# The products of p for the third and fourth column groups, moved behind their gates' products at the end of a one-core transformer block

## The chip, the cores and the metric

One core of a Trainium2 chip runs the whole program. The time is that of the device, in microseconds (us), for one execution. Of three timed runs of the kernel before, the median is 1574.86 us (1574.80 to 1574.87). The trace is of one further, profiled execution, which took 1574.96 us.

## The reference, cut to what matters

A decoder layer over 256 tokens and 2048 channels in float32: three token mixers, their gates and an output projection, then a gated MLP with a short convolution, and last a gated input embedding. Only the last step is touched, and the weights and products behind it:

```python
x = x + merged @ w_out[i]                                # (256, 2048)
h = rms_norm(x, norm_ffn_g[i])
u = causal_dwconv(h @ w_up[i], ffn_conv_w[i])
u_g, u_v = jnp.split(u, 2, axis=-1)
x = x + (jax.nn.silu(u_g) * u_v) @ w_down[i]
g = jax.nn.sigmoid(rms_norm(x, norm_ple_g[i]) @ w_ple_gate[i])   # (256, 2048) @ (2048, 2048)
x = x + g * (p[i] @ w_ple[i])                            # p: (256, 256), w_ple: (256, 2048)
```

The kernel computes the sigmoid as (1 + tanh(z/2)) / 2.

## The kernel before

All weights stream through a ring of four buffers in chunks of 128 partitions x 1024 columns (512 KB): two blocks of 128 input rows by 512 output columns. For each chunk c, in this order: SyncE issues its DMA into `raw` once chunk c-4 has been split (`chunk`, L334 to L340); ScalarE casts it to fp32r, `w_hi` (`high`, L894), once the DMA has landed and TensorE has used chunk c-4; VectorE computes the rest `w_lo = raw - w_hi` (`split`, L1215) and counts up `chunk_split`; TensorE waits for that count and runs 12 matmuls of 512 columns on it (`token_chunk`, L502 to L518: two token tiles x two row blocks x the products high-high, high-low, low-high), or 16 and 16 in the stages of the MLP's first projection, and counts up `chunk_used`.

Every engine runs its own list of instructions in the order in which the program is written. The lists are written by hand as loops over the chunk number: the work that belongs to a stage is put behind the cast or the split of a certain chunk. So a wait in such a piece of work holds up all later casts or splits of that engine.

A column group is 512 output columns; there are four. The products of a group are summed in one of two PSUM accumulators, `acc[number % 2]`, and the group two later in TensorE's order must wait until it has been read (`wait_taken`). The last stages are:

- Behind the output projection, near 735 us: four chunks "ple", one for each column group, with the products p @ w_ple. ScalarE copies each to SBUF, halved, into the tile `ple` (L954). `p_hi` and `p_lo` are the two parts of p, transposed.
- The MLP in two halves (UP1, DOWN1, UP2, DOWN2).
- From chunk PLEG on: four gate groups of eight chunks each with h @ w_ple_gate. END is the number of all chunks. Below, E-1 is the last chunk, E-2 the one before, and so on, so that a chunk can be named alike in both kernels. ScalarE takes the tanh of groups 0 to 2 behind a cast (L1174), that of group 3 for each token tile apart when its products are done (L1183). VectorE computes (tanh + 1) * ple into `fin` (L1704) and adds x (L1706); for group 3 tile by tile (L1711, L1713). `fin` has two buffers, for even and odd groups.
- SyncE issues the eight output DMAs (256 KB each, two for each column group) behind the DMAs of all weight chunks (L402). Each group's two count up `out_landed[g % 2]`. VectorE waits for the landing of group 0's output before it writes group 2's into the same buffer of `fin`.

## Time and profile before

| what | value |
|---|---|
| median of three timed runs | 1574.86 us |
| the profiled execution | 1574.96 us, its span 1573.0 us |
| TensorE matmuls busy | 1565.7 us, 100% of the span |
| VectorE busy | 1047.2 us, 67% |
| ScalarE busy | 780.9 us, 50% |
| chain that ended last | 99% TensorE |
| DMA | 297.16 MB, mean 189 GB/s |

The span is the time from the first to the last record of the profiled execution; 1.96 us of the execution's own time lie around it. Matmuls overlap, so a row with 390 ns for one is issued every 227 ns. Columns of a row of the timeline: start in us, length in us, engine, line, operation, out<-in, count, and in brackets the engine's idle time before it and what ended it.

### The profile page before, as it was taken

What the parts mean: (1) busy time and instruction counts of PE and PEld (TensorE: products, weight loads), DVE (VectorE), ACT (ScalarE), POOL (GpSimd) and SP (SyncE); (2) the same over time, 40 slices, a digit from 0 to 9 for tenths busy, and PEclk for the clock granted to TensorE, in tenths of its full rate; (3) what the DMA queues carried; (4) which work ended last, traced back from release to release, by engine and by line L of the source; (5) the groups of instructions that cost most, each with busy time, mean ns of one, the idle gap of its engine ahead of it and who ended that gap; (6) DMA issues with size and microseconds to landing.
All of it is one profiled execution on the core that took longest, in us unless ns stands there. A gap on an engine that the chain in (4) does not pass through costs nothing.

```text
span 1573.0 us, 21349 instructions
## 1 busy us (share of the span) xinstructions
PE 1565.7 (100%) x7740; PEld 1323.6 (84%) x7740; DVE 1047.2 (67%) x1238; ACT 780.9 (50%) x928; POOL 34.7 (2%) x53
## 2 busy tenths in 40 slices
PE   9999999999999999999999999999999999999998
PEld 7878888888888888888888888888888888888887
DVE  5699867765677556655677777764457777765554
ACT  7355454444554544455455555543345555544443
POOL 5000110000000000000000000000000000000000
PEclk9999999999999999999999999999999999999999
DMA  8656655665655666655666566656666666566564
GB/s 261 201 174 191 196 176 168 196 187 180 194 180 174 197 198 194 187 187 174 188 187 200 173 187 196 191 199 191 196 178 198 180 181 199 192 193 190 177 197 147
DMA packets 157074, 297.16 MB, mean 189 GB/s; under 512 B 9639, under 2 KB 14099, under 8 KB 157008
## 3 DMA queue, kind: packets, MB, share of 16 engines
q1 hardware_dynamic: 156464, 296.00, 61.3%
q8 instruction: 43, 0.70, 0.2%
q0 software_dynamic: 512, 0.27, 0.1%
q14 instruction: 23, 0.19, 0.0%
q10 hardware_dynamic: 32, 0.01, 0.0%
HBM read 294.14 MB, written 2.10 MB: 188 GB/s over the span
## 4 chain that ended last, share of the span: by engine, by line
PE 99%; DVE 0%; ACT 0%; issue 0%; POOL 0%; ACTq 0%; DVEq 0%; POOLq 0%
PE psum L513 21%; PE psum L515 21%; PE psum L514 21%; PE psum L486 20%; PE psum L492 11%; PE psum L678 0%; PE psum L625 0%; PE psum L579 0%; PE psum L689 0%; PE psum L712 0%; PE psum L534 0%; PE psum L647 0%; PE psum L666 0%; PE psum L656 0%; PE psum L568 0%
## 5 line engine op out<-in xcount | busy, mean ns | idle before, releaser
L1215 DVE TENSOR_TENSOR w_lo<-raw,w_hi 128x1024 fp32r<-128x1024 f32 x547 | 666.0, 1223 | 439.7 <-ACT w_hi L894 438.8
L894 ACT CAST w_hi<-raw 128x1024 fp32r<-128x1024 f32 x547 | 571.3, 1049 | 605.0 <-PE psum L515 461.7
L513 PE MATMUL psum<-w_hi,h_both 128*128 128x512 f32 x860 | 340.2, 396 | 0.0
L486 PE MATMUL psum<-h_both,w_hi 128*128 128x512 f32 x1408 | 336.4, 391 | 0.0
L515 PE MATMUL psum<-w_hi,h_both 128*128 128x512 f32 x860 | 335.1, 390 | 0.0
L514 PE MATMUL psum<-w_lo,h_both 128*128 128x512 f32 x860 | 335.0, 390 | 0.0
L486 PEld LDWEIGHTS psum<-h_both,w_hi 128*128 128x128 f32 x1408 | 258.7, 188 | 50.3 <-DVE rB L1595 0.3
L515 PEld LDWEIGHTS psum<-w_hi,h_both 128*128 128x128 f32 x860 | 161.5, 188 | 34.4
L513 PEld LDWEIGHTS psum<-w_hi,h_both 128*128 128x128 f32 x860 | 161.6, 188 | 33.0 <-issue 0.5
L514 PEld LDWEIGHTS psum<-w_lo,h_both 128*128 128x128 f32 x860 | 161.7, 188 | 31.9
L492 PEld LDWEIGHTS psum<-h_both,w_lo 128*128 128x128 f32 x1408 | 180.6, 191 | 6.9
L492 PE MATMUL psum<-h_both,w_lo 128*128 128x256 f32 x1408 | 182.9, 283 | 0.0
L513 PE MATMUL psum<-w_hi,f_hi 128*128 128x512 f32 x352 | 137.2, 390 | 0.0
L515 PE MATMUL psum<-w_hi,f_lo 128*128 128x512 f32 x352 | 137.0, 389 | 0.0
L514 PE MATMUL psum<-w_lo,f_hi 128*128 128x512 f32 x352 | 137.0, 389 | 0.0
L514 PEld LDWEIGHTS psum<-w_lo,f_hi 128*128 128x128 f32 x352 | 66.1, 188 | 13.7
L513 PEld LDWEIGHTS psum<-w_hi,f_hi 128*128 128x128 f32 x352 | 66.1, 188 | 13.7
L515 PEld LDWEIGHTS psum<-w_hi,f_lo 128*128 128x128 f32 x352 | 66.1, 188 | 13.6
L1304 DVE SCALAR_TENSOR_TENSOR val<-apad,cw,val 128x256 f32<-128x256 f32 x120 | 50.2, 480 | 1.0
L513 PE MATMUL psum<-w_hi,m_hi 128*128 128x512 f32 x128 | 50.2, 392 | 0.0
L514 PE MATMUL psum<-w_lo,m_hi 128*128 128x512 f32 x128 | 49.8, 389 | 0.0
L515 PE MATMUL psum<-w_hi,m_lo 128*128 128x512 f32 x128 | 49.8, 389 | 0.0
(274 smaller groups left out, 1079.1 us busy)
## 6 DMA issues: line engine op xcount, KB each, us to landing
raw<-in_w_up SPq DMA_DIRECT2D x176, 512.0 KB, 3.7
raw<-in_w_gate SPq DMA_DIRECT2D x96, 512.0 KB, 3.7
raw<-in_w_in SPq DMA_DIRECT2D x90, 512.0 KB, 3.7
raw<-in_w_down SPq DMA_DIRECT2D x88, 512.0 KB, 4.5
raw<-in_w_out SPq DMA_DIRECT2D x32, 512.0 KB, 3.8
raw<-in_w_ple_gate SPq DMA_DIRECT2D x32, 512.0 KB, 4.6
raw<-in_w_moba_out SPq DMA_DIRECT2D x16, 512.0 KB, 4.1
raw<-in_w_conv_out SPq DMA_DIRECT2D x8, 512.0 KB, 4.1
```

The source lines that it names most:

```text
L486: mm = nc.tensor.matmul(wide[part][:, j, :], w_hi[:, c % RING, w], h_both[:, kt + k, :, :].rearrange("p h s -> p (h s)"), start=first and ...
L492: mm = nc.tensor.matmul(wide[part][:, j, S:2 * S], w_lo[:, c % RING, w], h_hi[:, kt + k, :], start=False, stop=last and not low_first and ...
L513: nc.tensor.matmul(o, sh, w_hi[:, c % RING, w], start=first and k == 0, stop=False, skip_group_check=True)
L514: nc.tensor.matmul(o, sh, w_lo[:, c % RING, w], start=False, stop=False, skip_group_check=True)
L515: mm = nc.tensor.matmul(o, sl, w_hi[:, c % RING, w], start=False, stop=last and k == 1, skip_group_check=True)
L894: A.copy(w_hi[:, c % RING, :], raw[:, c % RING, :]).then_inc(chunk_high, 1)
L1215: V.tensor_tensor(w_lo[:, c % RING, :], raw[:, c % RING, :], w_hi[:, c % RING, :].bitcast(F32), ALU.subtract).then_inc(chunk_split, 1)
L1304: last = V.scalar_tensor_tensor(val[:, j, :], src, w, val[:, j, :], ALU.mult, ALU.add)
```

## The change

The loop over the "ple" chunks behind the output projection is cut from four groups to two (column groups 0 and 1). The chunks of w_ple for groups 2 and 3 now stand at the end: one behind the eight gate chunks of group 2 (`PLE2`, E-10) and one as the last chunk of the program (E-1). The number of chunks stays the same, so END is unchanged, PLEG and UP1 are two lower, and a chunk of the last stage that was PLEG+n is now PLEG+n+2 at the same place from the end. `GATE_AT` holds the first chunk of each gate group.

TensorE sums the moved products in the accumulator that follows their gate's; they are not copied out, but VectorE multiplies them in PSUM by the gate. For that, it first turns the tanh of groups 2 and 3 into the gate, (tanh + 1) * 0.5, in `gt2`, which has two buffers now. p's parts move to an address that stays free until the end; `ple` holds half its columns. On SyncE the loop with a register over the gate chunks becomes a written-out list.

```diff
@@ -68,7 +68,7 @@
                                 ("gv", 1, 8), ("gr", 1, 8), ("mq", 1, 8), ("mk", 1, 8),
                                 ("mq2", 1, 8), ("mk2", 1, 8), ("mv", 2, 8), ("yA", 4, 2),
                                 ("gA", 4, 8), ("yB", 4, 2), ("gB", 4, 8), ("yC", 4, 4),
-                                ("gC", 4, 8), ("wout", 4, 8), ("ple", 4, 1)):
+                                ("gC", 4, 8), ("wout", 4, 8), ("ple", 2, 1)):
         for g in range(count):
             GROUPS.append((name, g, c, chunks))
             c += chunks
...
@@ -82,7 +82,9 @@
 UP2 = DOWN1 + 4 * K1 // 2
 DOWN2 = UP2 + 16 * PAIRS2
 PLEG = DOWN2 + 4 * K2 // 2
-END = PLEG + 32
+PLE2 = PLEG + 24
+END = PLEG + 34
+GATE_AT = (PLEG, PLEG + 8, PLEG + 16, PLE2 + 1)
 GROUP_AT = {}
 for _n, (_name, _g, _c0, _k) in enumerate(GROUPS):
     for _j in range(_k):
...
@@ -210,8 +212,8 @@
     pT = ar("pT", [P, 2, 3 * P], 78)
     m_hi = ar("m_hi", [P, KD, S], 32, F32R)
     m_lo = ar("m_lo", [P, KD, S], 48, F32R)
-    p_hi = ar("p_hi", [P, 2, S], 64, F32R)
-    p_lo = ar("p_lo", [P, 2, S], 66, F32R)
+    p_hi = ar("p_hi", [P, 2, S], 80.5, F32R)
+    p_lo = ar("p_lo", [P, 2, S], 82.5, F32R)
     ptok = ar("ptok", [P, TT, PLE], 76)
     sqx = ar("sqx", [P, TT, W], 0)
     upg = ar("upg", [P, QD, 2 + S], 0)
...
@@ -221,8 +223,8 @@
     tg = ar("tg", [P, QD, S], 16.5)
     f_hi = ar("f_hi", [P, K1, S], 20.5, F32R)
     f_lo = ar("f_lo", [P, K1, S], 44.5, F32R)
-    ple = ar("ple", [P, TT, D], 68.5)
-    gt2 = ar("gt2", [P, TT, W], 8.5)
+    ple = ar("ple", [P, TT, 2 * W], 68.5)
+    gt2 = ar("gt2", [P, 2, TT, W], 8.5)
     fin = ar("fin", [P, 2, TT, W], 36.5)
 
     psum = nc.alloc_psum_tensor("psum", [P, 8, 512], F32)
...
@@ -390,11 +392,11 @@
         down(DOWN1, K1, 0)
         up(UP2, PAIRS2, PAIRS1)
         down(DOWN2, K2, K1)
-        with sp.Fori(0, 2) as i:
-            for half in range(2):
-                for j in range(8):
-                    chunk(PLEG + 8 * half + j,
-                          w_ple_gate[0][j * 256:(j + 1) * 256, bass.ds(i * 2 * W + half * W, W)], 2, i, 16)
+        for g in range(4):
+            for j in range(8):
+                chunk(GATE_AT[g] + j, w_ple_gate[0][j * 256:(j + 1) * 256, g * W:(g + 1) * W], 2)
+            if g >= 2:
+                chunk(GATE_AT[g] + 8, w_ple[0][:, g * W:(g + 1) * W], 2)
         for g in range(4):
             for t in range(TT):
                 if t == 0 or g == 3:
...
@@ -513,7 +515,7 @@
                     nc.tensor.matmul(o, sh, w_hi[:, c % RING, w], start=first and k == 0, stop=False, skip_group_check=True)
                     nc.tensor.matmul(o, sh, w_lo[:, c % RING, w], start=False, stop=False, skip_group_check=True)
                     mm = nc.tensor.matmul(o, sl, w_hi[:, c % RING, w], start=False, stop=last and k == 1, skip_group_check=True)
-                if c == END - 1 and t < TT - 1:
+                if c in (END - 2, END - 1) and t < TT - 1:
                     mm.then_inc(tile0_sums, 1)
             mm.then_inc(chunk_used, 1)
 
...
@@ -854,16 +856,27 @@
                 token_chunk(DOWN2 + g * n + j, number % 2, f_hi, f_lo, 2 * j, j == 0, j == n - 1)
                 if g and j == 1:
                     turn_x(g - 1, number - 1, U_X2 + g - 2 if g >= 3 else None)
-        for g in range(4):
-            number = NG_PLEG + g
+        def ple_gate(g, number):
+
             wait_taken(pe, number - 2)
             for j in range(8):
-                c = PLEG + 8 * g + j
                 if g == 0 and j % 2 == 0:
                     pe.wait_ge(unit_split, U_X2 + j // 2 + 1)
-                token_chunk(c, number % 2, h_hi, h_lo, 2 * j, j == 0, j == 7)
+                token_chunk(GATE_AT[g] + j, number % 2, h_hi, h_lo, 2 * j, j == 0, j == 7)
                 if g == 0 and j == 1:
                     turn_x(3, number - 1, U_X2 + 2)
+
+        def ple_sums(c, number):
+
+            wait_taken(pe, number - 2)
+            token_chunk(c, number % 2, p_hi, p_lo, 0, True, True)
+
+        ple_gate(0, NG_PLEG)
+        ple_gate(1, NG_PLEG + 1)
+        ple_gate(2, NG_PLEG + 2)
+        ple_sums(PLE2, NG_PLEG + 3)
+        ple_gate(3, NG_PLEG + 4)
+        ple_sums(END - 1, NG_PLEG + 5)
 
 
     @block.scalar
...
@@ -1168,19 +1181,19 @@
                     number = NG_PLEG + g
                     act.wait_ge(chunk_used, PLEG + 8 * g + 8)
                     act.wait_ge(r2_ready, 1)
-                    if g:
-                        act.wait_ge(pg_ready, g)
+                    if g == 2:
+                        act.wait_ge(pg_ready, 1)
                     for t in range(TT):
-                        last = A.activation(gt2[:, t, :], flat(acc[number % 2])[:, t * W:(t + 1) * W], ACT.Tanh,
+                        last = A.activation(gt2[:, g % 2, t, :], flat(acc[number % 2])[:, t * W:(t + 1) * W], ACT.Tanh,
                                             scale=small[:, 14 - t:15 - t])
                     last.then_inc(taken[number % 2], 1)
-        act.wait_ge(pg_ready, 3)
+        act.wait_ge(pg_ready, 2)
         for t in range(TT):
             if t == 0:
                 act.wait_ge(tile0_sums, 1)
             else:
-                act.wait_ge(chunk_used, END)
-            A.activation(gt2[:, t, :], flat(acc[(NG_PLEG + 3) % 2])[:, t * W:(t + 1) * W], ACT.Tanh,
+                act.wait_ge(chunk_used, GATE_AT[3] + 8)
+            A.activation(gt2[:, 1, t, :], flat(acc[(NG_PLEG + 4) % 2])[:, t * W:(t + 1) * W], ACT.Tanh,
                          scale=small[:, 14 - t:15 - t]).then_inc(tile_gate, 1)
 
 
...
@@ -1586,7 +1599,7 @@
                 if c == LAST["wout", g] + 5:
                     earlier()
                     x_low(g, U_X1 + g, R_FFN)
-            if c == UP1 + 1:
+            if c == UP1 + 3:
                 earlier()
                 x_mean(5)
             if c == UP1 + 10:
...
@@ -1694,22 +1707,38 @@
                 dve.wait_ge(rs_ready, 9)
                 V.tensor_scalar(small[:, 14:15], ms[:, 0:1], 0.5, None, ALU.mult)
                 V.tensor_scalar(small[:, 13:14], ms[:, 1:2], 0.5, None, ALU.mult).then_inc(r2_ready, 1)
-            for g in range(3):
+            for g in range(2):
                 if c == PLEG + 8 * g + (14 if g == 0 else 12):
                     number = NG_PLEG + g
                     cols = slice(g * W, (g + 1) * W)
                     wait_taken(dve, number)
-                    if g >= 2:
-                        dve.wait_ge(out_landed[g % 2], 16 * TT)
-                    V.scalar_tensor_tensor(fin[:, g % 2, :, :], gt2[:], 1.0, ple[:, :, cols], ALU.add, ALU.mult).then_inc(pg_ready, 1)
+                    V.scalar_tensor_tensor(fin[:, g, :, :], gt2[:, g, :, :], 1.0, ple[:, :, cols], ALU.add, ALU.mult).then_inc(pg_ready, 1)
                     dve.wait_ge(pg_ready, g + 1)
-                    V.tensor_tensor(fin[:, g % 2, :, :], fin[:, g % 2, :, :], xtok[:, :, cols], ALU.add).then_inc(out_ready, 1)
+                    V.tensor_tensor(fin[:, g, :, :], fin[:, g, :, :], xtok[:, :, cols], ALU.add).then_inc(out_ready, 1)
+            if c == PLEG + 28:
+                wait_taken(dve, NG_PLEG + 2)
+                V.tensor_scalar(gt2[:, 0, :, :], gt2[:, 0, :, :], 1.0, 0.5, ALU.add, ALU.mult).then_inc(gate_halved, 1)
+            if c == PLEG + 29:
+                cols = slice(2 * W, 3 * W)
+                dve.wait_ge(chunk_used, PLE2 + 1)
+                dve.wait_ge(gate_halved, 1)
+                dve.wait_ge(out_landed[0], 16 * TT)
+                V.tensor_tensor(fin[:, 0, :, :], tokens(acc[(NG_PLEG + 3) % 2]), gt2[:, 0, :, :], ALU.mult).then_inc(taken[(NG_PLEG + 3) % 2], 1)
+                wait_taken(dve, NG_PLEG + 3)
+                V.tensor_tensor(fin[:, 0, :, :], fin[:, 0, :, :], xtok[:, :, cols], ALU.add).then_inc(out_ready, 1)
         cols = slice(3 * W, 4 * W)
+        for t in range(TT):
+            dve.wait_ge(tile_gate, t + 1)
+            V.tensor_scalar(gt2[:, 1, t, :], gt2[:, 1, t, :], 1.0, 0.5, ALU.add, ALU.mult).then_inc(gate_halved, 1)
         dve.wait_ge(out_landed[1], 16 * TT)
         for t in range(TT):
-            dve.wait_ge(tile_gate, t + 1)
-            V.scalar_tensor_tensor(fin[:, 1, t, :], gt2[:, t, :], 1.0, ple[:, t, cols], ALU.add, ALU.mult).then_inc(pg_ready, 1)
-            dve.wait_ge(pg_ready, 4 + t)
+            if t == 0:
+                dve.wait_ge(tile0_sums, 2)
+            else:
+                dve.wait_ge(chunk_used, END)
+            dve.wait_ge(gate_halved, 2 + t)
+            V.tensor_tensor(fin[:, 1, t, :], flat(acc[(NG_PLEG + 5) % 2])[:, t * W:(t + 1) * W], gt2[:, 1, t, :], ALU.mult).then_inc(pg_ready, 1)
+            dve.wait_ge(pg_ready, 3 + t)
             V.tensor_tensor(fin[:, 1, t, :], fin[:, 1, t, :], xtok[:, t, cols], ALU.add).then_inc(out_ready, 1)
 
     block.__exit__(None, None, None)
```

What the diff does to VectorE's list around the wait for group 0's output, behind the additions of gate group 1 (L1706, after: L1717). The splits are L1215 before and L1228 after; `gt_118` is the tile `gt2`. Before:

```order
L1704 SCALAR_TENSOR_TENSOR fin<-gt_118,ple 128x1024 [waits taken1,chunk_split]
L1706 TENSOR_TENSOR fin<-fin,xtok 128x1024 [waits pg_ready]
L1215 TENSOR_TENSOR w_lo<-raw,w_hi 128x1024 [waits chunk_high]
L1215 TENSOR_TENSOR w_lo<-raw,w_hi 128x1024 [waits chunk_high,chunk_split] x7
L1704 SCALAR_TENSOR_TENSOR fin<-gt_118,ple 128x1024 [waits out_landed0,taken0,chunk_split]
L1706 TENSOR_TENSOR fin<-fin,xtok 128x1024 [waits pg_ready]
L1215 TENSOR_TENSOR w_lo<-raw,w_hi 128x1024 [waits chunk_high]
```

The wait for group 0's output stands behind E-4's split there. The same place in VectorE's list after:

```order
L1717 TENSOR_TENSOR fin<-fin,xtok 128x1024 [waits pg_ready]
L1228 TENSOR_TENSOR w_lo<-raw,w_hi 128x1024 [waits chunk_high]
L1228 TENSOR_TENSOR w_lo<-raw,w_hi 128x1024 [waits chunk_high,chunk_split] x7
L1720 TENSOR_SCALAR gt_118<-gt_118 128x1024 [waits taken0,chunk_split]
L1228 TENSOR_TENSOR w_lo<-raw,w_hi 128x1024 [waits chunk_high]
L1726 TENSOR_TENSOR fin<-psum,gt_118 128x1024 [waits gate_halved,out_landed0,chunk_used,chunk_split]
L1728 TENSOR_TENSOR fin<-fin,xtok 128x1024 [waits taken1]
L1228 TENSOR_TENSOR w_lo<-raw,w_hi 128x1024 [waits chunk_high]
```

Eight splits stand behind group 1's addition in both. Before, the eighth is that of E-4, and the wait on `out_landed0` follows with three splits behind it. Now the eighth is that of E-6, the halving follows, then one split (E-5), then the wait, with four splits behind it.

The end of VectorE's list before, from the last two splits on:

```order
L1215 TENSOR_TENSOR w_lo<-raw,w_hi 128x1024 [waits chunk_high,chunk_split] x2
L1711 SCALAR_TENSOR_TENSOR fin<-gt_118,ple 128x512 [waits chunk_split,out_landed1,tile_gate]
L1713 TENSOR_TENSOR fin<-fin,xtok 128x512 [waits pg_ready]
L1711 SCALAR_TENSOR_TENSOR fin<-gt_118,ple 128x512 [waits tile_gate]
L1713 TENSOR_TENSOR fin<-fin,xtok 128x512 [waits pg_ready]
```

Behind the tanh (`tile_gate`) there are two operations for each tile. The same end after, from the last three splits on (L1732 halves the gate, L1740 multiplies):

```order
L1228 TENSOR_TENSOR w_lo<-raw,w_hi 128x1024 [waits chunk_high,chunk_split] x3
L1732 TENSOR_SCALAR gt_118<-gt_118 128x512 [waits chunk_split,tile_gate]
L1732 TENSOR_SCALAR gt_118<-gt_118 128x512 [waits tile_gate]
L1740 TENSOR_TENSOR fin<-psum,gt_118 128x512 [waits gate_halved,tile0_sums,out_landed1]
L1742 TENSOR_TENSOR fin<-fin,xtok 128x512 [waits pg_ready]
L1740 TENSOR_TENSOR fin<-psum,gt_118 128x512 [waits gate_halved,chunk_used]
L1742 TENSOR_TENSOR fin<-fin,xtok 128x512 [waits pg_ready]
```

Two operations for each token tile stood behind the tanh; now the tanh and the halving of both tiles stand ahead of the two operations that follow the last products.

SyncE's list before, at the last weight chunks and the first outputs (ISA is an instruction that only waits; REGISTER_ALU computes the next address or count):

```order
L339 ISA [waits chunk_split]
L339 DMA raw<-in_w_ple_gate 128x2x512
L336 REGISTER_ALU
L339 ISA [waits chunk_split]
L339 DMA raw<-in_w_ple_gate 128x2x512
L393 REGISTER_ALU
L393 COMPARE_AND_BRANCH
L402 DMA out<-fin 128x512 [waits out_ready]
L402 DMA out<-fin 128x512
L402 DMA out<-fin 128x512 [waits out_ready]
```

Each weight DMA has a waiting instruction and a register step of its own. SyncE's list at the same place after:

```order
L384 COMPARE_AND_BRANCH
L341 DMA raw<-in_w_ple_gate 128x2x512 [waits chunk_split] x24
L341 DMA raw<-in_w_ple 128x2x512 [waits chunk_split]
L341 DMA raw<-in_w_ple_gate 128x2x512 [waits chunk_split] x8
L341 DMA raw<-in_w_ple 128x2x512 [waits chunk_split]
L404 DMA out<-fin 128x512 [waits out_ready]
L404 DMA out<-fin 128x512
L404 DMA out<-fin 128x512 [waits out_ready]
```

The loop's registers and its branch are gone, and the DMA of the last w_ple chunk stands directly ahead of the outputs.

## Rows read from the trace of the kernel before

**Rows 1.** The page: the span, and busy time of TensorE.
```profile
span 1573.0 us, 21349 instructions
...
PE 1565.7 (100%) x7740; PEld 1323.6 (84%) x7740; DVE 1047.2 (67%) x1238; ACT 780.9 (50%) x928; POOL 34.7 (2%) x53
```

**Rows 2.** The timelines of four engines at the end of the span.
```profile
1567.52 0.39 PE L515 MATMUL psum<-w_hi,h_both 128*128 128x512 f32 x1
...
1566.67 0.69 ACT L1183 ACTIVATE gt<-psum,small 128x512 f32<-128x512 f32 x1 [8.67 <-PE psum L515]
1567.94 0.69 ACT L1183 ACTIVATE gt<-psum,small 128x512 f32<-128x512 f32 x1 [0.59 <-PE psum L515]
...
1567.49 0.69 DVE L1711 SCALAR_TENSOR_TENSOR fin<-gt,ple 128x512 f32<-128x512 f32 x1 [5.58 <-ACT gt L1183]
1568.21 0.69 DVE L1713 TENSOR_TENSOR fin<-fin,xtok 128x512 f32<-128x512 f32 x1
...
1569.54 0.69 DVE L1713 TENSOR_TENSOR fin<-fin,xtok 128x512 f32<-128x512 f32 x1
...
1570.26 0.33 SPq L402 DMA_DIRECT2D out<-fin  x1
```

**Rows 3.** The timeline of VectorE, from E-5's split to the last splits.
```profile
1547.22 1.23 DVE L1215 TENSOR_TENSOR w_lo<-raw,w_hi 128x1024 fp32r<-128x1024 f32 x1 [1.49 <-ACT w_hi L894]
1549.91 1.23 DVE L1215 TENSOR_TENSOR w_lo<-raw,w_hi 128x1024 fp32r<-128x1024 f32 x1 [1.47 <-ACT w_hi L894]
1555.77 1.23 DVE L1704 SCALAR_TENSOR_TENSOR fin<-gt,ple 128x1024 f32<-128x1024 f32 x1 [4.64 <-DMA out<-fin]
1557.03 1.22 DVE L1706 TENSOR_TENSOR fin<-fin,xtok 128x1024 f32<-128x1024 f32 x1
1558.17 3.74 DVE L1215 TENSOR_TENSOR w_lo<-raw,w_hi 128x1024 fp32r<-128x1024 f32 x3
```

**Rows 4.** The timeline of the matmuls and weight loads, at the starts of E-4 and E-3.
```profile
1556.66 0.39 PE L513 MATMUL psum<-w_hi,h_both 128*128 128x512 f32 x1
...
1559.44 0.19 PEld L513 LDWEIGHTS psum<-w_hi,h_both 128*128 128x128 f32 x1 [0.32 <-DVE w_lo L1215]
...
1559.79 0.39 PE L514 MATMUL psum<-w_lo,h_both 128*128 128x512 f32 x1
```

**Rows 5.** The groups by line and shape, a VectorE operation reading PSUM.
```profile
L1428 DVE TENSOR_SCALAR ex<-psum 128x512 f32<-128x512 f32 x1 | 0.7, 692 | 0.0
```

**Rows 6.** SyncE's queue: E-1's weights, then the second output of group 0.
```profile
1548.61 0.37 SPq L339 DMA_DIRECT2D raw<-in_w_ple_gate  x1
...
1549.61 0.42 SPq L402 DMA_DIRECT2D out<-fin  x1
```

**Rows 7.** The timelines of VectorE and SyncE in a written-out stretch near 725 us.
```profile
723.26 1.23 DVE L1215 TENSOR_TENSOR w_lo<-raw,w_hi 128x1024 fp32r<-128x1024 f32 x1 [1.49 <-ACT w_hi L894]
...
724.51 0.37 SPq L339 DMA_DIRECT2D raw<-in_w_ple  x1
```

**Rows 8.** The DMA view; KB, us to landing: issues at 1549.19, 1549.61, 1550.57, 1558.28.
```profile
out<-fin SPq DMA_DIRECT2D x1, 256.0 KB, 4.3
...
out<-fin SPq DMA_DIRECT2D x1, 256.0 KB, 6.0
...
out<-fin SPq DMA_DIRECT2D x1, 256.0 KB, 6.4
...
out<-fin SPq DMA_DIRECT2D x1, 256.0 KB, 2.4
```

**Rows 9.** The timeline of ScalarE, at the tanh of gate group 2.
```profile
1546.06 1.05 ACT L894 CAST w_hi<-raw 128x1024 fp32r<-128x1024 f32 x1 [1.67 <-PE psum L515]
1547.15 1.27 ACT L1174 ACTIVATE gt<-psum,small 128x512 f32<-128x512 f32 x2
```

**Rows 10.** Stretches after TensorE's last matmul; the third figure from the end: the granted clock.
```profile
1568.00:1572.00 4.00, 0.00 (x0) 0.00 (x0) 2.17 (x4) 0.63 (x1) 0.00 (x0) 1.00 0.34 131
1572.00:1573.00 1.00, 0.00 (x0) 0.00 (x0) 0.00 (x0) 0.00 (x0) 0.00 (x0) 0.87 0.00 0
```

More of the change, by code:

```diff
@@ L277, in trunk @@
     r2_ready, pg_ready, out_ready = sem("r2_ready"), sem("pg_ready"), sem("out_ready")
-    tile0_sums, tile_gate = sem("tile0_sums"), sem("tile_gate")
+    tile0_sums, tile_gate, gate_halved = sem("tile0_sums"), sem("tile_gate"), sem("gate_halved")
     cv_ready = sem("cv_ready")
```

## The prediction

> **What bounds the kernel now.** I read the page first: TensorE is busy for 1565.7 us of a span of 1573.0 us [rows 1]. Every microsecond taken from another engine is worth nothing unless TensorE waits for it, or it stands behind the last matmul. So two questions decide: does TensorE run through after the change as it does before, and what is left behind its last matmul?
>
> The tail first. The last matmul starts at 1567.52. The tanh of the second token tile starts at 1567.94, VectorE's last addition at 1569.54, and the last output is issued at 1570.26: 2.74 us from the last matmul's start to the issue [rows 2].
>
> Then VectorE's timeline in the last 26 us [rows 3]. Normally it idles 1.49 us ahead of each split, waiting for the cast. After the split of E-4 (1549.91 to 1551.14) it waits 4.64 us for the landing of group 0's output, then multiplies and adds for group 2, and only at 1558.17 goes on to the splits of E-3, E-2 and E-1, 3.74 / 3 = 1.25 us each. E-3's split ends at 1559.42. In TensorE's rows [rows 4] E-4 starts at 1556.66. From the second matmul of E-3 (1559.79) to the last of all (1567.52) are 34 matmuls, 0.2273 us each, or 2.73 us for a chunk of 12. E-3's second matmul was due at 1556.66 + 13 x 0.2273 = 1559.62 and comes at 1559.79, and its weight load has 0.32 us idle ahead of it, put down to the split. So before, the long wait of VectorE already costs TensorE 0.17 us: the cover of three split chunks is used to the last bit.
>
> **The change, part by part.**
>
> TensorE's products: 24 matmuls leave the place behind the output projection and 24 come in at the end, of the same shape. Sum 0. ScalarE loses two copies, VectorE gains halvings: none of it on the path unless shown below. Behind the output projection ScalarE and VectorE do the same work at the same distance from its last chunk, less the two copies; only the MLP's first chunks stand two places nearer. I take 0, with 0 to +1 us as bounds, since one of those chunks could now be wanted before it is split.
>
> The wait on `out_landed0`. This is the term that counts. SyncE issues group 0's output behind E-1's weights, and those wait for E-5's split: the same in both kernels. The landing is therefore at nearly the same time. But VectorE now comes to this wait one split earlier: E-4's split stands behind it, not ahead of it. Queued behind the waiting multiplication are E-4's to E-1's splits, and TensorE waits for the first of them.
>
> Its time: VectorE starts the multiplication at 1555.77 in the trace. Multiplication and addition are both 128x1024 as before; the multiplication now reads PSUM. A 128x512 operation reading PSUM took 0.692 us [rows 5], as long as the 0.69 us of those at the end of VectorE's list that read SBUF [rows 2], so the price is the same. The first split behind them ends at 1559.42, as before, if the landing is the same.
>
> The landing can be a little earlier, because SyncE's loop is written out. In the loop E-1's DMA is issued at 1548.61 [rows 6], 0.16 us after E-5's split ended (1547.22 + 1.23 = 1548.45) [rows 3]; in a written-out stretch the lag is 724.51 - 724.49 = 0.02 us [rows 7]. The second output of group 0 was issued at 1549.61, 1.00 us after E-1's weights; with DMAs of 0.37 and 0.42 us in a row and no branch it would be some 0.8 us. So it is issued 0.14 + 0.2 = 0.34 us earlier, its weights ahead of it 0.14 us. It landed 6.0 us after its issue [rows 8], behind the weights and beside group 1's outputs, so not all of it comes back. Bounds 0 and 0.34; I take 0.25.
>
> So E-4's split ends at 1559.42 - 0.25 = 1559.17. E-3's load came at 1559.44, 0.02 us behind its split, and the second matmul 0.35 us behind the load [rows 4]. So E-4's second matmul comes at 1559.54. It is due at 1556.66 + 0.23 = 1556.89. TensorE loses 2.65 us, against the 0.17 us it loses now: +2.48 us. The later splits are ahead again (1.25 us each against 2.73 us).
>
> Both ends of this term: if the landing is as late as the slowest output of these rows (6.4 us) [rows 8] and SyncE gains nothing, 0.4 + 0.25 more: +3.1 us. If both outputs land like the one that had nothing beside it (2.4 us behind an issue at 1549.3, so 1551.7), the split of E-4 ends at 1551.8 + 1.26 + 1.14 + 1.25 = 1555.4, ahead of E-4's load, and the term is -0.17 us. I take +2.48, since the 6.0 us is of this very DMA with the same traffic ahead and beside it.
>
> The page "DMA: Bandwidth & Descriptors" of the Trainium skill (section "Anatomy of one DMA — SWDGE (gpsimd) path") gives a transfer a fixed part of about 2 us and a part by its bytes; for 256 KB that is an estimate of 2.6 us, for another kind of queue. The rows agree with it for the output that had nothing beside it (2.4 us), and disagree for group 0's (4.3 and 6.0 us). By the page the wait would be gone by 1552 and the change a gain; by the rows it isn't.
>
> The tanh of group 2. Gate group 3 (its first chunk is E-9) now uses the accumulator of group 2, not of group 1, since the p products of group 2 stand between. So E-9's first load waits for the tanh behind E-7's cast. In the trace the pair of tanhs stands behind E-5's cast, 1547.15 to 1548.42 [rows 9]; two chunks earlier it ends at 1542.97. E-9 starts at 1556.66 - 5 x 2.73 = 1543.0, its load is due 0.2 us ahead of that. TensorE would lose some 0.1 us; bounds 0 and 0.2. It shifts the later casts with it, so it isn't hidden by the later wait: +0.1 us.
>
> The halving of group 2, one operation of 128x1024, stands between two splits with 1.49 us idle ahead of each [rows 3]. It is not in the trace; a 128x512 operation took 0.69 us [rows 5], a two-operand one of 128x1024 1.23 us [rows 3]. Both ends fit into the 1.49 us: 0 us. If that cover were gone it would delay E-5's split and with it E-1's weights and the landing.
>
> The tail. Counted from the last matmul's start: the first tile's sums are ready for another engine 0.85 us before it (1567.52 - 1566.67), the second's 0.42 us after it (1567.94) [rows 2]. VectorE multiplies tile 0 at -0.85 and adds at -0.13 (dependent operations stand 0.72 us apart: 1567.49, 1568.21). The multiplication of tile 1 needs its products (+0.42) and VectorE (+0.48 to +0.5, since the 1.33 us from 1568.21 to 1569.54 hold one operation and a dependent one, 0.61 + 0.72). So it starts at +0.5, the addition at +1.22, the output's issue 0.72 us later, at +1.94. Before it was +2.74: -0.8 us. The tanhs and halvings of group 3 lie beside the 2.73 us of E-1: tanh of tile 1 from about -2.3 to -1.6, halving done by about -0.8, just as tile 0's multiplication wants VectorE. Bounds -0.6 and -0.85.
>
> The sum: +2.48 + 0.1 - 0.8 = +1.8 us (rounded) on the profiled execution's 1574.96 us, that is 1576.7 us (1573.0 + 1.8 = 1574.8 of span and 1.96 us around it). The median of the runs shown is 0.1 us below the profiled execution, so I predict 1576.6 us, 0.11% above 1574.86. A difference within 0.2% (3.15 us) is about what this kernel's measurement can't tell from no change.
>
> **The rivals.**
>
> A, the output lands early, and TensorE doesn't wait. For it: outputs with nothing beside them took 2.4 us; against it: both of group 0 were issued directly behind 512 KB of weights, here as there, and took 4.3 and 6.0 us. With 4.3 us from 1549.3, VectorE starts at 1553.7, E-4's split ends at 1557.35, and TensorE loses 0.83 us: 0.83 - 0.17 + 0.1 - 0.8, the same time as before, 1574.8. With 2.4 us: 1573.9. The change then does what it can at the tail and nothing else.
>
> B, TensorE's clock falls in the gap: slower than before beyond the measurement. TensorE stands still for some 2.65 us in front of E-4. What the trace shows: behind the last matmul, which ends at 1567.9, the granted clock stays at its full level, 2.4 GHz, over 1568 to 1572, and is 0.87 over the last microsecond, that is, it fell to 1.2 GHz for the last quarter of it, some 4.8 us after the last matmul [rows 10]. A gap of 2.65 us is shorter, and that speaks against B; that a fall may come sooner in another execution speaks for it. The price: a chunk at half the clock takes 2.73 us more; one to four chunks are +2.7 to +10.9 us, so 1579.3 to 1587.5. It decides from the first chunk on.
>
> The section "HAM oscillation — how this bites in real kernels" of "TensorE: Matmul & The Clock Gate" in the Trainium skill warns of this: idle gaps between groups of matmuls make the next group start at the low clock. The rows show only the fall at the span's end, after a longer silence than this gap.
>
> C, something is late behind the output projection, where the MLP's first chunks now follow two chunks sooner on the additions, squares and transposes of x. For it: it is the other place whose distances change. Against it: TensorE is not busy for 7.3 us of the span [rows 1], 5.1 us of them behind its last matmul (1573.0 - 1567.9), so it hardly waits anywhere else, and two copies fall away from ScalarE's list. Price up to one chunk, +2.7 us: 1579.3.
>
> **How the numbers follow.** My forecast, the gap of 2 to 3.2 us: 0.76, its own range 1576.0 to 1577.4. A: 0.12, 1573.9 to 1575.5. B: 0.07. C: 0.05. The range that leaves out B, most of C and the best of A is 1574.5 to 1578.5. Slower by over 0.2% (above 1578.0): B, C and a little of my own, 0.12. Faster by over 0.2% (below 1571.7): no case reaches it, 0.02 for what I have not seen. Within 0.2%: 0.86.
>
> **What the profile of the changed kernel would show.** Right: a gap of TensorE of about 2.6 us ahead of E-4's first weight load, released by the split; VectorE idle for about 7 us, from 1548.5 to 1555.5, ended by the DMA of the output; no 4.6 us idle time behind E-4's split; last matmul near 1570.1; one multiplication and one addition between it and the last output's issue, 1.9 us in all. Wrong: the output of group 0 landing before 1553; a granted clock under 1.0 before the last microsecond; TensorE gaps near 742 to 765 us; a halving over 1.5 us. If the gap is there and the time isn't, the landing was mis-sized; if there is no gap, A is right.

## The result and the profile after

The changed kernel's median is 1577.55 us, against 1574.86 us before (22 runs each). One of the changed kernel's runs took 2635.63 us at a granted clock of 0.556, a disturbed state that the others don't show; it is in the median of 22 and not in the ratio, and without it the median is 1577.06 us. The ratio is 1.0016, 95% interval [1.0011, 1.0022]: slower, by less than the 0.2% that I called no change, though the interval reaches just beyond it. The profiled execution took 1576.56 us, its span 1574.5 us.

The median alone misleads. The other 21 runs stand in two groups: eleven from 1576.24 to 1577.06 us and ten from 1578.03 to 1579.84 us, with nothing between. So a median stands at an edge of the empty stretch or in it (1577.55 us is the mean of 1577.06 and 1578.03), and one or two runs more or less in a group would move it by 1 us. The kernel before has 22 runs from 1574.61 to 1575.31 us. The granted clock, a mean over the run, is 1.000 or 0.999 in the lower group and 0.997 to 0.999 in the upper; by itself it does not tell a run's group.

The profile after is of the lower group. The view of TensorE's waits has one new row, ahead of three that stand at the start of the span:

```profile
PE psum L515 <- DVE w_lo L1228: 2.3, 1, 2.3
PE psum L570 <- POOL ident L414: 1.5, 1, 1.5
```

The timelines of the weight loads and matmuls around E-4 answer to [rows 4]:

```profile
1559.07 0.19 PEld L515 LDWEIGHTS psum<-w_hi,h_both 128*128 128x128 f32 x1 [2.74 <-DVE w_lo L1228]
...
1556.36 0.39 PE L517 MATMUL psum<-w_hi,h_both 128*128 128x512 f32 x1
1559.07 0.50 PE L515 MATMUL psum<-w_hi,h_both 128*128 128x512 f32 x1 [2.32 <-DVE w_lo L1228]
1559.41 0.39 PE L516 MATMUL psum<-w_lo,h_both 128*128 128x512 f32 x1
```

E-4 was due 0.23 us behind the matmul at 1556.36, its second matmul at 1556.82; it comes at 1559.41, 2.59 us late, where before E-3's was 0.17 us late. The timeline of VectorE answers to [rows 3]:

```profile
1544.30 1.23 DVE L1228 TENSOR_TENSOR w_lo<-raw,w_hi 128x1024 fp32r<-128x1024 f32 x1 [1.47 <-ACT w_hi L907]
1545.56 0.69 DVE L1720 TENSOR_SCALAR gt<-gt 128x1024 f32<-128x1024 f32 x1
1547.07 1.23 DVE L1228 TENSOR_TENSOR w_lo<-raw,w_hi 128x1024 fp32r<-128x1024 f32 x1 [0.82 <-ACT w_hi L907]
1555.40 1.23 DVE L1726 TENSOR_TENSOR fin<-psum,gt 128x1024 f32<-128x1024 f32 x1 [7.10 <-DMA out<-fin]
1556.66 1.23 DVE L1728 TENSOR_TENSOR fin<-fin,xtok 128x1024 f32<-128x1024 f32 x1
1557.80 4.99 DVE L1228 TENSOR_TENSOR w_lo<-raw,w_hi 128x1024 fp32r<-128x1024 f32 x4
```

The wait is 7.10 us instead of 4.64 us, because it starts one split sooner and ends at nearly the same time (1555.40, before 1555.77); four splits stand behind it instead of three. The end of the span answers to [rows 2]; the last row is SyncE's:

```profile
1568.29 0.43 DVE L1732 TENSOR_SCALAR gt<-gt 128x512 f32<-128x512 f32 x1 [0.75 <-ACT gt L1196]
1568.98 0.69 DVE L1740 TENSOR_TENSOR fin<-psum,gt 128x512 f32<-128x512 f32 x1 [0.27 <-PE psum L517]
1569.71 0.69 DVE L1742 TENSOR_TENSOR fin<-fin,xtok 128x512 f32<-128x512 f32 x1
1570.32 0.68 DVE L1740 TENSOR_TENSOR fin<-psum,gt 128x512 f32<-128x512 f32 x1
1571.04 0.69 DVE L1742 TENSOR_TENSOR fin<-fin,xtok 128x512 f32<-128x512 f32 x1
...
1569.86 0.39 PE L517 MATMUL psum<-w_hi,p_lo 128*128 128x512 f32 x1
...
1571.76 0.33 SPq L404 DMA_DIRECT2D out<-fin  x1
```

From the last matmul's start to the last output's issue it is 1571.76 - 1569.86 = 1.90 us, before 2.74 us. This is the gain of the change, 0.84 us, and it is there in full.

### The profile page after: what moved, and what is told of

Same layout as the page of the kernel before. It is cut to its first block, busy times and chain, and to the rows that moved or that the text cites. A ratio compares the mean times of both kernels' runs of the same rounds, so it can differ in the third digit from the quotient of the medians.

```text
span 1574.5 us, 21237 instructions
## 1 busy us (share of the span) xinstructions
PE 1565.3 (99%) x7740; PEld 1322.9 (84%) x7740; DVE 1048.4 (67%) x1241; ACT 779.1 (49%) x926; POOL 34.6 (2%) x53
## 4 chain that ended last, share of the span: by engine, by line
PE 98%; DVE 1%; DMA 0%; ACT 0%; issue 0%; SPq 0%; POOL 0%; ACTq 0%; DVEq 0%; POOLq 0%
PE psum L515 21%; PE psum L517 21%; PE psum L516 21%; PE psum L488 20%; PE psum L494 11%; PE psum L680 0%; PE psum L627 0%; PE psum L581 0%; DMA out<-fin 0%; PE psum L691 0%; DVE w_lo L1228 0%; PE psum L714 0%; PE psum L536 0%; PE psum L649 0%; PE psum L668 0%
## 5 line engine op out<-in xcount | busy, mean ns | idle before, releaser
L1228 DVE TENSOR_TENSOR w_lo<-raw,w_hi 128x1024 fp32r<-128x1024 f32 x547 | 665.8, 1223 | 438.6 <-ACT w_hi L907 438.1
```

Source lines behind the costliest of these rows:

```text
L1228: V.tensor_tensor(w_lo[:, c % RING, :], raw[:, c % RING, :], w_hi[:, c % RING, :].bitcast(F32), ALU.subtract).then_inc(chunk_split, 1)
```

## The experiments

Each was timed with the kernel before on the same chip, whose medians there were 1574.95, 1574.89 and 1575.05 us. The theory has two parts: TensorE's gap is E-4's split standing behind VectorE's wait for the landing; and the upper group of runs are those in which the clock falls in that gap (the last two profiles will show it falling just behind it). Rivals: the new operations or accumulators cost the time, and the upper group is a later landing.

**The wait one split later.**

```diff
-            if c == PLEG + 29:
+            if c == PLEG + 30:
                 cols = slice(2 * W, 3 * W)
```

> One edit on the changed kernel: the multiplication of group 2 with its wait for the output's landing stands behind E-4's split again, not behind E-5's. Theory (the gap of TensorE is one split that stands behind the wait): TensorE's 2.7 us gap ahead of E-4 goes and about 0.2 us ahead of E-3 come back, as in the kernel before; 1576.5 - 2.5 = 1574.0 to 1574.2 us, 0.8 us under the kernel before, and runs near 1578.5 us disappear with the gap. Rival (the gap's price is made by the multiplication reading PSUM or by the accumulator that is freed later): the time stays at 1576 or more, with a gap at E-1.

Measured: 1574.13 us, 11 runs from 1574.07 to 1574.51, all under the 33 runs of before on this chip (1574.68 to 1575.60); ratio 0.9994 [0.9985, 1.0003]. Its timelines:

```profile
1556.04 1.23 DVE L1726 TENSOR_TENSOR fin<-psum,gt 128x1024 f32<-128x1024 f32 x1 [4.75 <-DMA out<-fin]
...
1559.71 0.19 PEld L515 LDWEIGHTS psum<-w_hi,h_both 128*128 128x128 f32 x1 [0.47 <-DVE w_lo L1228]
```

VectorE waits until the same time (1556.04), but with E-4's split ahead of the wait, TensorE is held only at E-3, by a gap of 0.47 us between loads. One number in the program takes back the whole loss, and both groups with it. That the multiplication reads PSUM and frees its accumulator later costs nothing.

**A third buffer, no wait.** Group 2's multiplication keeps its new place.

```diff
-    fin = ar("fin", [P, 2, TT, W], 36.5)
+    fin = ar("fin", [P, 3, TT, W], 36.5)
...
-                dve.wait_ge(out_landed[0], 16 * TT)
-                V.tensor_tensor(fin[:, 0, :, :], tokens(acc[(NG_PLEG + 3) % 2]), gt2[:, 0, :, :], ALU.mult).then_inc(taken[(NG_PLEG + 3) % 2], 1)
+                V.tensor_tensor(fin[:, 2, :, :], tokens(acc[(NG_PLEG + 3) % 2]), gt2[:, 0, :, :], ALU.mult).then_inc(taken[(NG_PLEG + 3) % 2], 1)
```

In lines not shown, the addition and the output DMA use the third buffer too.

> Two edits on the changed kernel: group 2's result goes into a third buffer, and its wait for group 0's output is gone; its place in VectorE's list stays. Theory (the landing alone ends VectorE's wait): no gap of TensorE at all in the last 30 us but 0.1 us at E-9, so 1573.8 to 1574.0 us, 0.2 us under the kernel whose wait stands one split later. Rival (VectorE would be late anyway, for the halving and the multiplication are new work ahead of E-4's split): a gap of 0.5 us or more stays, over 1574.5 us.

Measured: 1574.08 us (1573.92 to 1574.19, 11 runs), ratio 0.9994 [0.9985, 1.0003]. VectorE's timeline:

```profile
1547.32 1.23 DVE L1228 TENSOR_TENSOR w_lo<-raw,w_hi 128x1024 fp32r<-128x1024 f32 x1 [0.82 <-ACT w_hi L907]
1548.59 1.22 DVE L1725 TENSOR_TENSOR fin<-psum,gt 128x1024 f32<-128x1024 f32 x1
1549.84 1.22 DVE L1727 TENSOR_TENSOR fin<-fin,xtok 128x1024 f32<-128x1024 f32 x1
1550.99 1.22 DVE L1228 TENSOR_TENSOR w_lo<-raw,w_hi 128x1024 fp32r<-128x1024 f32 x1
```

The new work between the splits is hidden: E-4's split ends at 1552.2, more than 4 us before TensorE wants it. The place is harmless; the landing made it dear. The further 0.2 us that I expected under the last experiment did not come: the two medians differ by 0.05 us.

**The kernel before with a third buffer.** Group g of 0 to 2 is written to `fin[:, g, ...]`, the wait is gone (the lines for the buffer's size, the addition and the output DMA are not shown):

```diff
-                    if g >= 2:
-                        dve.wait_ge(out_landed[g % 2], 16 * TT)
-                    V.scalar_tensor_tensor(fin[:, g % 2, :, :], gt2[:], 1.0, ple[:, :, cols], ALU.add, ALU.mult).then_inc(pg_ready, 1)
+                    V.scalar_tensor_tensor(fin[:, g, :, :], gt2[:], 1.0, ple[:, :, cols], ALU.add, ALU.mult).then_inc(pg_ready, 1)
```

> The kernel before with a third buffer for group 2's result, so without its wait of 4.64 us for the landing. Theory (that wait costs TensorE only 0.17 us ahead of E-3): 1574.86 - 0.17 = 1574.7 us, and VectorE idle behind E-4's split no longer. Rival (the wait hid more, such as the late splits at the end): under 1574.4 us.

Measured: 1574.91 us (1574.65 to 1575.16, 11 runs) against 1574.95 us, ratio 0.9999 [0.9990, 1.0008]. The wait of 4.64 us is gone and moves nothing that can be measured. The 0.17 us that I read from the rows is neither confirmed nor refuted: the medians differ by 0.04 us, the single runs by 0.5 us.

**The kernel before with its wait one split sooner.** Nothing of the change is in it.

```diff
-                if c == PLEG + 8 * g + (14 if g == 0 else 12):
+                if c == PLEG + 8 * g + (14, 12, 11)[g]:
```

> One edit on the kernel before: group 2's multiplication, with its wait for the landing, stands behind E-5's split instead of E-4's. Nothing else of the change is in it. Theory (the place of this wait against the splits is the whole cost): a gap of 2.5 to 2.9 us ahead of E-4, lower group at 1574.9 + 2.6 = 1577.4 to 1577.7 us, and about half the runs 2 us above that. Rival (moving p's products or the accumulators is part of the cost): under 1577 us.

Measured: five runs from 1577.40 to 1577.96 and six from 1578.81 to 1579.29 us, median 1578.81, ratio 1.0022 [1.0013, 1.0031]. Its profile, of the lower group, shows the gap:

```profile
1555.54 1.23 DVE L1704 SCALAR_TENSOR_TENSOR fin<-gt,ple 128x1024 f32<-128x1024 f32 x1 [7.22 <-DMA out<-fin]
...
1559.21 0.19 PEld L513 LDWEIGHTS psum<-w_hi,h_both 128*128 128x128 f32 x1 [2.93 <-DVE w_lo L1215]
```

One split's place makes, in the old kernel, the loss and the two groups. Its lower group lies 2.5 to 3.1 us above 1574.89: the changed kernel's loss without its gain at the tail. Its upper group lies only 1.1 us above the lower (medians 1578.94 and 1577.85), not the 2 us that I expected; I have no trace of an upper run of it.

**Group 0's outputs issued earlier.** SyncE's two DMAs of group 0 stand behind the weights of E-6, not of E-1:

```diff
+        def write_out(g):
             for t in range(TT):
...
+                if g == 3 and j == 3:
+                    for k in (0,):
+                        write_out(k)
...
+        for g in (1, 2, 3):
+            write_out(g)
```

> One edit on the changed kernel: SyncE issues group 0's two outputs ahead of the last five chunks' weights, right behind E-6's, instead of behind E-1's. Theory (VectorE waits because the outputs are issued so late and behind weights): they land by about 1547, VectorE's wait is gone, no gap of TensorE, 1574.0 to 1574.2 us, as with the third buffer. Rival (outputs in front delay the weights behind them, so TensorE waits for a chunk's cast): over 1574.6 us, with a gap of TensorE released by the cast.

Measured: 1574.07 us (1573.88 to 1574.34, and one run at 1575.14), ratio 0.9995 [0.9986, 1.0004]. VectorE doesn't wait for a landing:

```profile
1547.16 1.23 DVE L1233 TENSOR_TENSOR w_lo<-raw,w_hi 128x1024 fp32r<-128x1024 f32 x1 [0.82 <-ACT w_hi L912]
1548.42 1.23 DVE L1731 TENSOR_TENSOR fin<-psum,gt 128x1024 f32<-128x1024 f32 x1
```

The outputs took 4.8 and 6.6 us there too, from 1535.2 on, where nobody waits for them. TensorE has no gap for late weights.

**Group 1's outputs behind group 2's.** The order of SyncE's outputs is 0, 2, 1, 3:

```diff
-        for g in range(4):
+        def write_out(g):
             for t in range(TT):
...
+        for g in (0, 2, 1, 3):
+            write_out(g)
```

> One edit on the changed kernel: group 1's outputs are issued behind group 2's, so that only E-1's weights are ahead of group 0's outputs and nothing is beside them. Theory (group 1's 512 KB beside them make the difference between 2.4 and 6.0 us): the second output of group 0 lands about 1.0 us earlier, after some 5 us or less, the gap of TensorE shrinks to 1.4 to 1.8 us, the time to 1575.3 to 1575.7 us, and no run is near 1578.5 us, since the gap is short. Rival (the landing is set by the weights ahead alone): 1576.5 us as before, with both groups.

Measured: five runs from 1575.91 to 1577.18 and six from 1578.02 to 1578.70 us, ratio 1.0017 [1.0008, 1.0026]. My theory of the landing falls. VectorE's wait (in the stretches behind it, the last three figures are the granted clock, the busy share of the DMA engines, and GB/s):

```profile
1556.05 1.22 DVE L1731 TENSOR_TENSOR fin<-psum,gt 128x1024 f32<-128x1024 f32 x1 [7.22 <-DMA out<-fin]
```

The stretches:

```profile
1554.00:1555.00 1.00, 1.00 (x6) 0.84 (x5) 0.00 (x0) 0.33 (x1) 0.00 (x0) 1.00 0.13 51
1555.00:1556.00 1.00, 1.00 (x7) 0.81 (x6) 0.00 (x0) 0.73 (x1) 0.00 (x0) 1.00 0.07 27
```

The traffic is all but over by 1554 (some 78 KB are moved in these two us, worked out from their GB/s), since 512 KB fewer are under way, and yet the output lands at 1556. So the 6 us are not the sharing of the engines with group 1's outputs. Outputs issued behind weights took 4.3 to 6.6 us in four kernels, those with no weights ahead 2.3 to 3.4 us. The busy stretch ends some 2 us before the landing, not far from what an output with no weights ahead takes in all; that would fit outputs whose data stand behind the weights', but no run here tests it.

**The gap filled.** Nine small matmuls of 128 columns (`keep_busy`) with an unread result stand in front of E-4; each leaves two records in the trace:

```diff
+                if g == 3 and j == 5:
+                    keep_busy(9)
                 token_chunk(GATE_AT[g] + j, number % 2, h_hi, h_lo, 2 * j, j == 0, j == 7)
```

> One edit on the changed kernel: nine small matmuls of 0.25 us each, whose result nobody reads, stand ahead of E-4's in TensorE's list, so they fill 2.25 us of its gap. Theory (the runs near 1578.5 us are those in which TensorE's clock fell after the gap): the gap is filled, the time of the lower group stays, 1576.3 to 1576.8 us, and no run is near 1578.5 us; the clock is 1.000 in all. Rival (the upper group comes from a landing that is later in some runs, or from the change's place in the ring): both groups stay, about half the runs near 1578.5 us.

Measured: 1576.63 us, 11 runs from 1576.12 to 1577.07, none above; ratio 1.0009 [1.0000, 1.0018]. TensorE's rows:

```profile
1556.89 2.17 PE L570 MATMUL psum<-ones 128*128 128x128 f32 x18
1559.38 0.53 PE L515 MATMUL psum<-w_hi,h_both 128*128 128x512 f32 x1 [0.32 <-DVE w_lo L1230]
```

E-4 still waits for its split, and starts at 1559.38, no sooner than in the profile after (1559.07), so the landing was no earlier; the upper group is gone. VectorE's multiplication starts at 1555.71 there, behind a wait of 7.12 us (profile after: 7.10). Had the upper group been runs with a later landing, the small matmuls would have left it in place; that cause is ruled out.

**The gap half filled.** The same with `keep_busy(4)`.

> As the filled gap, but with four of the small matmuls in place of nine: they fill 1.0 us and leave some 1.6 us. Theory (the fall depends on how long TensorE stands still): fewer runs near 1578.5 us than the 10 of 21 of the changed kernel, 0 to 3 of 11, the others at 1576.2 to 1577 us. Rival (any filling helps, or the filling in the last experiment helped by its place in front of the gap and not by its length): none at all, or as many as without it.

Measured: 1576.82 us, 11 runs from 1576.29 to 1576.95, none above; ratio 1.0011 [1.0002, 1.0020].

```profile
1556.67 1.06 PE L570 MATMUL psum<-ones 128*128 128x128 f32 x8
1559.29 0.50 PE L515 MATMUL psum<-w_hi,h_both 128*128 128x512 f32 x1 [1.56 <-DVE w_lo L1230]
```

1.56 us of standing still remained, and by their times no run of 11 lost its clock. Whether a shorter gap or any work inside it helps, this run cannot tell: both expected few or none.

**The gap longer.** VectorE does one more operation ahead of E-4's split:

```diff
+                V.tensor_tensor(ple[:], xtok[:, :, 0:2 * W], xtok[:, :, 2 * W:4 * W], ALU.add)
                 wait_taken(dve, NG_PLEG + 3)
```

> One edit on the changed kernel: VectorE adds two halves of x into a tile that nobody reads any more (128x2048, some 2.3 us) between group 2's multiplication and addition, so TensorE's gap ahead of E-4 grows from 2.7 to 5.0 us. Theory (the clock falls in part of the runs because the gap is just short of always enough): every run now has the fall, the granted clock is 1.2 GHz in the stretch behind the gap, and the time is 1576.5 + 2.3 + about 2 = 1580.5 to 1581.5 us in all runs. Rival (the two groups of the changed kernel have another cause, such as the landing): two groups again, 1578.8 and 1580.8 us, at a granted clock of 1.0 in the rows behind the gap.

Measured: 1581.43 us, five runs from 1580.45 to 1581.93; ratio 1.0042 [1.0028, 1.0055]. The first matmuls behind the gap:

```profile
1561.49 0.64 PE L515 MATMUL psum<-w_hi,h_both 128*128 128x512 f32 x1 [4.45 <-DVE w_lo L1228]
1561.92 0.63 PE L516 MATMUL psum<-w_lo,h_both 128*128 128x512 f32 x1
1562.35 0.63 PE L517 MATMUL psum<-w_hi,h_both 128*128 128x512 f32 x1
```

The stretches of the same run:

```profile
1556.00:1561.00 5.00, 1.05 (x5) 0.55 (x3) 5.00 (x4) 1.04 (x1) 0.00 (x0) 1.00 0.02 6
1561.00:1564.00 3.00, 2.51 (x6) 2.01 (x7) 2.90 (x4) 0.00 (x0) 0.00 (x0) 0.62 0.46 175
1564.00:1567.00 3.00, 3.00 (x12) 2.42 (x11) 1.22 (x1) 0.00 (x0) 0.00 (x0) 0.81 0.00 0
1567.00:1570.00 3.00, 3.00 (x15) 2.48 (x14) 0.00 (x0) 0.00 (x0) 0.00 (x0) 1.00 0.00 0
```

Behind the gap the matmuls are 0.43 us apart instead of 0.23: TensorE runs at 1.2 GHz, and is back at 2.4 GHz by 1565.2. The granted clock is still 1.00 up to 1561.0, so here it fell in the last 0.5 us of the gap. This trace is of the fastest of the five runs, which is 2.3 + 1.6 us above 1576.56; the other four have no trace, but are 1.0 to 1.5 us slower still, so by their times every run has the fall. Their further 1 us is more than I expected (two are above 1581.5) and stays unexplained.

**Two more profiles of the changed kernel.** No edit.

> The changed kernel once more, for one more profile; with some luck it is one of the upper group, near 1578.5 us. Theory (the clock falls in the gap): in such a run the first matmuls behind the gap are 0.43 us apart as behind the longer gap, for about 3 us, and the granted clock of that stretch is near 0.5; in a run near 1576.5 us they are 0.23 us apart. Rival (a later landing): in a run near 1578.5 us the gap is 4.7 us long and all matmuls are 0.23 us apart.

> The same kernel and the same expectation, for a second profile: near 1578.5 us the theory wants matmuls 0.43 us apart behind a gap of 2.7 us, the rival a gap of 4.7 us.

Measured: 1578.78 and 1578.31 us, both of the upper group. Here the kernel before is at 1575.05 us, 0.2 us above its 1574.86 beside the first runs. The second's matmuls behind the gap:

```profile
1559.30 0.50 PE L515 MATMUL psum<-w_hi,h_both 128*128 128x512 f32 x1 [2.44 <-DVE w_lo L1228]
1559.64 0.48 PE L516 MATMUL psum<-w_lo,h_both 128*128 128x512 f32 x1
1559.92 0.63 PE L517 MATMUL psum<-w_hi,h_both 128*128 128x512 f32 x1
1560.34 0.63 PE L515 MATMUL psum<-w_hi,h_both 128*128 128x512 f32 x1
```

Its stretches:

```profile
1556.00:1559.00 3.00, 0.86 (x4) 0.38 (x2) 2.97 (x3) 1.05 (x1) 0.00 (x0) 1.00 0.02 8
1559.00:1562.00 3.00, 2.70 (x7) 2.13 (x8) 2.90 (x4) 0.00 (x0) 0.00 (x0) 0.63 0.45 171
```

And the same stretch of the lower group's profile, of the same kernel:

```profile
1559.00:1562.00 3.00, 2.93 (x13) 2.43 (x14) 2.90 (x4) 0.00 (x0) 0.00 (x0) 1.00 0.38 141
```

The gap is nearly as long (2.44 against 2.32 us), VectorE's wait 7.22 against 7.10 us; what differs is the clock. From the matmul at 1559.64 to the ninth behind it (1563.28) it is 3.64 us, and 2.07 us for the same nine in the lower group's profile (1559.41 to 1561.48): the slow clock costs 1.57 us. That is most of the 1.75 us between 1578.31 and 1576.56; the rest is within the 0.2 us by which the kernel before is slower here.

The clock does not fall in the gap, as the theory had it, but behind it: the granted clock is 1.00 over 1556 to 1559, the first matmul is as long as in the lower group's profile, and only the second is slowed. The first of the two profiles shows it more clearly:

```profile
1559.70 0.50 PE L515 MATMUL psum<-w_hi,h_both 128*128 128x512 f32 x1 [2.82 <-DVE w_lo L1228]
...
1560.74 0.49 PE L516 MATMUL psum<-w_lo,h_both 128*128 128x512 f32 x1
1561.03 0.63 PE L517 MATMUL psum<-w_hi,h_both 128*128 128x512 f32 x1
```

The fall comes in the fifth matmul behind the gap, 1.0 us after the gap's end, and costs 1.6 us as well. The landing was later in this run (VectorE's wait is 7.60 us) and the gap 0.5 us longer, which makes up the rest of its time. The length of the gap does not tell the groups apart: the traced gaps without the fall are 2.3 to 2.5 us long (this kernel and the two others with two groups), those with it 2.44 and 2.82 us. What decides it in one execution no run shows.

## Why the prediction was right, and where it was not

**The time** was inside the range, 0.95 us above the point (0.46 us by the median of 21). The profiled execution, 1576.56 us, is what the sum said (1576.7); the median is not, because the sum had no term for the clock. That it stayed inside is in part luck: with a few more falls the median would have stood in the upper group, above 1578.0 us: over the 0.2% and close to the end of the range.

**The wait on `out_landed0`**, +2.48 us: right. VectorE starts the multiplication at 1555.40 (1555.52 foretold), E-4's second matmul is 2.59 us late (2.65). The written-out loop on SyncE gives what was read from [rows 7]. Moving one place in VectorE's list does it both ways, in the changed kernel and in the old one.

**The tanh of group 2**, +0.1 us: right in size. E-9's load has 0.22 us idle ahead of it, put down to the tanh, and its second matmul comes 0.07 us late (1543.19, due at 1543.12).

**The halving**, 0: right; it took 0.69 us for 128x1024, the lower of my two ends, hidden in the 1.49 us ahead of the split, of which 0.82 stay.

**The tail**, -0.8 us: 0.84 measured, with the halving of tile 1 done at 1568.72, ahead of the multiplication at 1568.98.

**Behind the output projection**, 0: right. TensorE is busy for all of 735 to 765 us in the new trace, and rival C did not occur.

**Rival A**, the early landing, did not occur: outputs issued behind weights landed late, as in the rows before. Why they do I had wrong in the experiment on it, where I named the traffic beside them. By its own terms A's best case was 1574.0 us (-0.17 + 0.1 - 0.8 on 1574.86), not 1573.9.

**Rival B** is where the prediction failed: "A gap of 2.65 us is shorter, and that speaks against B", and its chance of 0.07. The clock fell in 12 of 23 executions of the changed kernel (two of the 12 by a trace, ten by their times; the run at 2635.63 us isn't counted). A single fall seen in a trace, behind 4.8 us of silence, says that this much suffices and nothing on how little does. The section "HAM oscillation — how this bites in real kernels" of "TensorE: Matmul & The Clock Gate" in the Trainium skill says that idle gaps between groups of matmuls start the next group at the low clock; the waits of the kernel that it shows are longer than this gap. The runs here show the fall for about every second gap of 2.3 to 2.8 us, and not always with the first matmul. Had I given B the half that it deserved, with the price that the runs show, the forecast would have been 1576.7 or 1578.5, and the range 1576 to 1579. The price was off as well: I said 2.7 to 10.9 us, a full chunk at half the clock as the least; it is 1.6 us in each of the three traces that have the fall, and 1.95 us between the groups' medians (1576.56 and 1578.51), since the clock comes back within less than a chunk's worth of matmuls. The chances did not quite add up either: B and C alone are the 0.12 for over 1578.0 us, and nothing is left for "a little of my own".

The forecast of no measurable change held at its edge, with B's price taking it close: 0.17% above by the medians, 0.16% by the ratio, the interval reaching 0.22%.

The three versions without the gap are below both kernels: 1574.07 to 1574.13 us, 0.8 to 0.9 us under the kernel before on the same chip. This is the tail's 0.84 us. Their intervals reach 1.0003 or 1.0004 and so don't exclude no change, but of their 33 runs 32 are faster than the fastest of 27 or 33 of before.

## What to carry to other kernels

When work is added to a hand-written list, read what every wait in it now stands ahead of: an engine with a third of its time free can still hold up the one that bounds the kernel, if the next thing that engine needs is queued behind a wait for a DMA. A wait for a buffer whose output is still on its way cost nothing measurable here until a split that TensorE needed stood behind it; a third buffer or an earlier issue takes the wait away without touching the order. And where a gap opens in TensorE's work, look at every run's time and not only at the median: the clock may fall in half of them.

## What the hardware showed that I had not expected

After a gap of TensorE of 2.3 to 2.8 us the clock fell to 1.2 GHz in about half of the executions (12 of 23 of the changed kernel, 6 of 11 of each of two others, most of them told by their times), after one of 4.45 us in five of five (one traced), after one of 1.56 us (with four small matmuls ahead of it) in none of eleven. The fall needn't come in the gap: in both traced runs of the upper group it came behind it, once in the second matmul and once in the fifth.

An output of 256 KB took 4.3 to 6.6 us behind weights and 2.3 to 3.4 us without them, and this didn't shrink when the traffic beside it was taken away and the DMA engines were busy for only 0.13 and 0.07 of the last two us before the landing. What holds it stays open.

A VectorE tensor_scalar from SBUF with constants took 0.69 us for 128x1024 and 0.43 us for 128x512, where two-operand operations of the same sizes take 1.23 and 0.69 us.
